# Half products for every second pair of slabs in the FFN up projection, with weight sums made by adding DMAs

## The reference

```python
def conv_ffn(x, w_up, conv_w, conv_b, w_down):
    h = x @ w_up                     # 512 x 1024 @ 1024 x 5632
    h = conv over 3 tokens, per channel, causal, + conv_b
    gate, val = jnp.split(h, 2, axis=-1)
    return (jax.nn.silu(gate) * val) @ w_down
...
x = x + rms_norm(conv_ffn(rms_norm(x, pre_ffn), *ffns[i]), post_ffn)
```

## Time and profile before

| what | value |
|---|---|
| runs | median 2073.37 us of 3 (2070.84 to 2076.74) |
| the profiled execution | 2073.53 us, its span 2071.8 us |
| granted TensorE clock | 0.998 of full speed |
| PE | 2053.4 us busy, 99% of the span |
| DVE | 1413.2 us, 68% |
| ACT | 1023.9 us, 49% |
| POOL | 398.3 us, 19% |
| chain that ended last | PE 85%, DVE 9%, ACT 2%, DMA 2%, issue 1% |
| four stretches of up projection | 165 to 405, 655 to 870, 1220 to 1440 and 1716 to 1935 us, DMA 28% to 32% busy |
| start of the down projection | 405 to 480 us: DVE 69.58 of 75 us busy, DMA 77% |

### The profile page before, as it was taken

How to read it: one execution, slowest core, us unless ns; L and a number is a source line. 1 busy time by engine, 2 the same in 40 slices (tenths; PEclk the granted TensorE clock), 3 DMA queues, 4 the chain that set the end, 5 groups by cost and what they waited for, 6 DMA issues and landing times.

```text
span 2071.8 us, 32448 instructions
## 1 busy us (share of the span) xinstructions
PE 2053.4 (99%) x11724; PEld 1728.4 (83%) x11724; DVE 1413.2 (68%) x2250; ACT 1023.9 (49%) x1671; POOL 398.3 (19%) x454
## 2 busy tenths in 40 slices
PE   9999999999999999999999999999999999999998
PEld 8889888888988888888877898888878889888886
DVE  5665555999366555699788655456987666554897
ACT  4754333557334433456556644334565764333555
POOL 0520211310000121120045401212200520121220
PEclk9999999999999999999999999999999999999999
DMA  8123322384430332267421113233674131233383
GB/s 287 63 102 102 100 88 95 120 262 157 143 132 31 102 101 92 90 189 244 156 72 42 62 41 104 99 101 96 193 229 163 63 103 60 87 98 101 105 265 117
DMA packets 73881, 251.62 MB, mean 121 GB/s; under 512 B 8448, under 2 KB 12672, under 8 KB 73392
## 3 DMA queue, kind: packets, MB, share of 16 engines
q1 hardware_dynamic: 58752, 213.10, 31.2%
q0 software_dynamic: 7168, 16.78, 3.7%
q10 hardware_dynamic: 7856, 20.34, 2.8%
HBM read 248.04 MB, written 6.34 MB: 123 GB/s over the span
## 4 chain that ended last, share of the span: by engine, by line
PE 85%; DVE 9%; ACT 2%; DMA 2%; issue 1%; POOL 0%; DVEq 0%; ACTq 0%; SPq 0%; POOLq 0%
PE ps L2011 16%; PE ps L2013 16%; PE ps L2012 16%; PE ps L2196 6%; PE ps L2530 4%; PE ps L2532 4%; PE ps L2531 4%; PE ps L2083 2%; DMA raw<-slabs 2%; DVE w_lo L1352 2%; PE ps L2039 2%; PE ps L2041 2%; PE ps L2040 2%; PE ps L2071 1%; PE ps L2055 1%; PE ps L2056 1%
## 5 line engine op out<-in xcount | busy, mean ns | idle before, releaser
L2011 PE MATMUL ps<-h_hi,w_hi 128*128 128x512 f32 (+1 forms) x1552 | 606.6, 391 | 0.0
L2012 PE MATMUL ps<-h_lo,w_hi 128*128 128x512 f32 (+1 forms) x1552 | 603.2, 389 | 0.0
L2013 PE MATMUL ps<-h_hi,w_lo 128*128 128x512 f32 (+1 forms) x1552 | 603.2, 389 | 0.0
L1747 DVE SCALAR_TENSOR_TENSOR work<-ps,conv_sb,work 128x511 f32<-128x511 f32 (+1 forms) x352 | 246.2, 744 | 379.4 <-ACT work L1138 379.2
L1352 DVE TENSOR_TENSOR w_lo<-raw,w_hi 128x1024 fp32r<-128x1024 f32 x356 | 439.1, 1240 | 43.6 <-ACT w_hi L777 39.9
L777 ACT ACTIVATE w_hi<-raw 128x1024 fp32r<-128x1024 f32 x368 | 384.5, 1051 | 129.9 <-DVE raw L1836 71.8
L1138 ACT ACTIVATE work<-ps,conv_sb 128x512 f32<-128x512 f32 x176 | 137.0, 778 | 474.7 <-PE ps L2013 445.5
L2011 PEld LDWEIGHTS ps<-h_hi,w_hi 128*128 128x128 f32 x1552 | 291.4, 188 | 62.6 <-issue 4.0
L2013 PEld LDWEIGHTS ps<-h_hi,w_lo 128*128 128x128 f32 x1552 | 291.3, 188 | 60.5
L2012 PEld LDWEIGHTS ps<-h_lo,w_hi 128*128 128x128 f32 x1552 | 291.5, 188 | 58.6
L718 POOL TENSOR_TENSOR bias<-act 128x256 f32<-128x256 f32 x40 | 78.7, 1967 | 996.4 <-DVE act L1753 996.4
(11 more groups left out here) (289 smaller groups left out, 3367.5 us busy)
## 6 DMA issues: line engine op xcount, KB each, us to landing
raw<-slabs SPq DMA_DIRECT2D x368, 512.0 KB, 3.8
act<-slabs POOLq DMA_DIRECT2D x64, 256.0 KB, 5.5
bias<-slabs SPq DMA_DIRECT2D x16, 512.0 KB, 6.1
act<-slabs SPq DMA_DIRECT2D x12, 512.0 KB, 5.7
bias_dram<-bias_rows ACTq DMA_DIRECT2D x2, 2048.0 KB, 13.3
g_post<-gains ACTq DMA_DIRECT2D x8, 512.0 KB, 4.9
bias<-bias_dram ACTq DMA_DIRECT2D x2, 2048.0 KB, 9.6
g_pre<-gains ACTq DMA_DIRECT2D x7, 512.0 KB, 6.9
```

The source lines that it names most:

```text
L1747: ve.scalar_tensor_tensor(y, ps[:, 2 * par + e, 0:SEQ - sh], conv_sb[:, L, t, tap:tap + 1], y, ALU.mult, ALU.add).then_inc(done, 1)
L2011: pe.matmul(ps[:, bank, cols], hi, h_hi[:, k, cols], start=k == 0, stop=False)
L2012: pe.matmul(ps[:, bank, cols], hi, h_lo[:, k, cols], start=False, stop=False)
L2013: last = pe.matmul(ps[:, bank, cols], lo, h_hi[:, k, cols], start=False, stop=k == KT - 1)
```

## The change

In each layer the pairs q = 4, 6, ..., 16 (seven of 22) are made by seven half products. A pair's weights are seen as a 2 x 2 block matrix (output row: gate or value slab; column: first or second half of the 1024 features), the input as 2 x 2 blocks (half of the features; half of the tokens). A half product is 4 k-tiles x 3 matmuls with 256 columns. PE makes them in the order a11, a12, x2, x1, x3, then the whole ordinary slab (q+1, 0), then a22, x4, then the ordinary slab (q+1, 1). This group of two pairs is a `period`. Some products are added onto others in PSUM, so earlier states are copied out by ACT (`copy` 0, 1, 2, 128x256 each) and added back by DVE (`c11`, `c22`, `c12`).

Four sums of weights are needed. DVE makes x2 in SBUF; x1, x3 and x4 are made by DMAs issued by POOL that add onto `raw`: x1 and x3 read the slab from DRAM again, x4 reads x2's place in SBUF. Four differences of the input (`join`, `differ`) are made by DVE at the start of each layer's up projection, split by ACT and DVE (`in_high`, `in_low`) and kept, two of them in the place of x. So x is written to DRAM before (four DMAs of 512 KB on ACT's queue) and read back after pair 18's silu (four more). `down_sums` is called once in each period and not as soon as its pairs are gated. The loops of the stage are written out.

```diff
+FAST, FAST_END = 4, 18
+FASTS = (FAST_END - FAST) // 2
+PARTS = "a11", "x1", "x2", "x3", "x4"
...
-                ring_slabs(n1 + EARLY, DOWN[L] + FFT)
+                ring_slabs(n1 + EARLY, up_slab(L, FAST))
+                for q in range(FAST, FAST_END + 2, 2):
+                    for e in range(2):
+                        c = up_slab(L, q, e)
+                        if q == FAST:
+                            sp.wait_ge(lo_made, made(c - RAW))
+                        elif e:
+                            sp.wait_ge(part_lo_made["x3"], fast(L, q - 2) + 1)
+                            sp.wait_ge(part_lo_made["x4"], fast(L, q - 2) + 1)
+                        else:
+                            sp.wait_ge(part_lo_made["x1"], fast(L, q - 2) + 1)
+                            sp.wait_ge(up_x2, fast(L, q - 2) + 1)
+                        sp.dma_start(raw[:, raw_slot(c), :], slabs[dram(c)]).then_inc(raw_in[raw_slot(c)], 16)
+                    if q < FAST_END:
+                        for e in range(2):
+                            c = up_slab(L, q + 1, e)
+                            sp.wait_ge(lo_made, made(c - RAW))
+                            sp.dma_start(raw[:, raw_slot(c), :], slabs[dram(c)]).then_inc(raw_in[raw_slot(c)], 16)
+                ring_slabs(up_slab(L, FAST_END + 1), DOWN[L] + FFT)
...
+            def up_sums(L):
+
+                def x1(q):
+                    even = up_slab(L, q)
+                    slot = raw_slot(even)
+                    pool.wait_ge(raw_in[slot], raw_count(even))
+                    pool.dma_start(raw[:, slot, 0:SEQ], slabs[dram(even)][:, SEQ:D], accum_op=ALU.add).then_inc(x1_in, 16)
+
+                def x3_x4(q):
+                    row1 = raw_slot(up_slab(L, q, 1))
+                    pool.wait_ge(part_lo_made["a11"], fast(L, q) + 1)
+                    pool.wait_ge(up_x2, fast(L, q) + 1)
+                    pool.dma_start(raw[:, row1, 0:SEQ], slabs[dram(up_slab(L, q))][:, 0:SEQ], accum_op=ALU.add).then_inc(x3_in, 16)
+                    pool.dma_start(raw[:, row1, SEQ:D], sum_place(), accum_op=ALU.add).then_inc(x4_in, 16)
+
+                x1(FAST)
+                for q in range(FAST, FAST_END, 2):
+                    x3_x4(q)
+                    if q + 2 < FAST_END:
+                        x1(q + 2)
+                    down_sums(L, (q - FAST) // 2)
+                for j in range(FASTS, STEPS - 1):
+                    down_sums(L, j)
...
+                def copy(q, n):
+
+                    if n == 2:
+                        sc.wait_ge(w_used, up_slab(L, q) + 2)
+                    else:
+                        sc.wait_ge(up_mm, 5 * fast(L, q) + (1, 3)[n])
+                    if q > FAST:
+                        sc.wait_ge(up_c, 3 * fast(L, q - 2) + (1, 3, 2)[n])
+                    sc.activation(kept_sum(n), ps[:, up_bank(q, 0), 0:HALF], ACT.Copy).then_inc(up_copy, 1)
...
+                def in_high(n):
+
+                    sc.wait_ge(in_sum, 8 * L + 5 + n)
+                    sc.wait_ge(x_out, 16 * TT * (L + 1))
+                    hi, _ = in_parts(n)
+                    sc.activation(hi, whole(*IN_PLACES[n]), ACT.Copy).then_inc(in_hi, 1)
...
+                def period(q):
+
+                    i = q // 2
+                    tap(1, i - 1, 1)
+                    split_hi(up_slab(L, q + 1))
+                    silu(1, i - 1)
+                    copy(q, 0)
+                    part_hi(q, "x3")
+                    split_hi(up_slab(L, q + 1, 1))
+                    copy(q, 1)
+                    part_hi(q, "x4")
+                    copy(q, 2)
+                    if q + 2 < FAST_END:
+                        part_hi(q + 2, "a11")
+                        part_hi(q + 2, "x2")
+                        fast_tap(q, 0)
+                        part_hi(q + 2, "x1")
+                        fast_tap(q, 1)
+                    else:
+                        fast_tap(q, 0)
+                        sc.wait_ge(up_mm, 5 * fast(L, q) + 5)
+                        split_hi(up_slab(L, q + 2))
+                        fast_tap(q, 1)
+                        split_hi(up_slab(L, q + 2, 1))
+                    silu(0, i)
+                    tap(1, i, 0)
...
+                for t in range(TT):
+                    sc.wait_ge(xn_made, TT * (2 * L + 1) + t + 1)
+                    sc.dma_start(x_dram[t], x[:, t, :]).then_inc(x_out, 16)
                 end = FFT // 2 - 1
-                for c in range(2):
-                    pair(c)
-                with sc.Fori(1, end - 1) as i:
-                    for c in range(2):
-                        pair(c, i)
+                pair(0)
+                pair(1)
+                for n in range(4):
+                    in_high(n)
+                tap(0, 1, 0)
+                part_hi(FAST, "x1")
+                tap(0, 1, 1)
+                part_hi(FAST, "a11")
+                silu(0, 1)
+                part_hi(FAST, "x2")
+                tap(1, 1, 0)
+                for q in range(FAST, FAST_END, 2):
+                    period(q)
+                tap(1, end - 2, 1)
+                split_hi(up_slab(L, FAST_END + 1))
+                silu(1, end - 2)
+                split_hi(up_slab(L, FAST_END + 1, 1))
                 pair(0, end - 1)
+                sc.wait_ge(w_used, up_slab(L, FAST_END))
+                for t in range(TT):
+                    sc.dma_start(x[:, t, :], x_dram[t]).then_inc(x_back, 16)
...
+                def period(q):
+
+                    i = q // 2
+                    slab_taps(q - 1, 1)
+                    split_lo(up_slab(L, q + 1))
+                    gate(1, i - 1)
+                    part_lo(q, "x3")
+                    split_lo(up_slab(L, q + 1, 1))
+                    c11(q)
+                    part_lo(q, "x4")
+                    c22(q)
+                    if q + 2 < FAST_END:
+                        x2(q + 2)
+                        part_lo(q + 2, "a11")
+                        part_lo(q + 2, "x2")
+                        slab_taps(q, 0)
+                        c12(q)
+                        part_lo(q + 2, "x1")
+                        slab_taps(q, 1)
+                    else:
+                        slab_taps(q, 0)
+                        c12(q)
+                        split_lo(up_slab(L, q + 2))
+                        slab_taps(q, 1)
+                        split_lo(up_slab(L, q + 2, 1))
+                    gate(0, i)
+                    slab_taps(q + 1, 0)
...
                 end = FFT // 2 - 1
-                for c in range(2):
-                    pair(c)
-                with ve.Fori(1, end - 1) as i:
-                    for c in range(2):
-                        pair(c, i)
+                for n in range(4):
+                    join(n)
+                pair(0)
+                differ(0)
+                differ(1)
+                pair(1)
+                differ(2)
+                differ(3)
+                in_low(0)
+                in_low(1)
+                in_low(2)
+                x2(FAST)
+                taps(0, 1)
+                part_lo(FAST, "x1")
+                gate(0, 1)
+                part_lo(FAST, "a11")
+                in_low(3)
+                part_lo(FAST, "x2")
+                slab_taps(FAST - 1, 0)
+                for q in range(FAST, FAST_END, 2):
+                    period(q)
+                slab_taps(FAST_END - 1, 1)
+                split_lo(up_slab(L, FAST_END + 1))
+                gate(1, end - 2)
+                split_lo(up_slab(L, FAST_END + 1, 1))
...
-                with pe.Fori(1, FFT // 2) as i:
-                    for c in range(2):
-                        pair(c, i)
-
+                def product(q, e, half, name, operand, begin, onto=False):
+                    o = ps[:, up_bank(q, e), HALF * half:HALF * (half + 1)]
+                    (hi, lo), (b_hi, b_lo) = up_parts(L, q, name), operand
+                    for k in range(KT // 2):
+                        w = slice(k * P, (k + 1) * P)
+                        pe.matmul(o, hi[:, w], b_hi[:, k, :], start=begin and k == 0, stop=False, skip_group_check=onto)
+                        pe.matmul(o, hi[:, w], b_lo[:, k, :], start=False, stop=False, skip_group_check=onto)
+                        last = pe.matmul(o, lo[:, w], b_hi[:, k, :], start=False, stop=k == KT // 2 - 1, skip_group_check=onto)
+                    return last
+
+                for c in range(2):
+                    pair(c, 1)
+                for q in range(FAST, FAST_END, 2):
+                    even, f = up_slab(L, q), fast(L, q)
+                    if q >= FAST + 4:
+                        pe.wait_ge(tap0, UP_SLABS * L + 2 * (q - 4) + 2)
+                    pe.wait_ge(part_lo_made["a11"], f + 1)
+                    product(q, 0, 0, "a11", h_quarter(0, 0), True).then_inc(up_mm, 1)
+                    product(q, 1, 0, "a12", h_quarter(1, 0), True).then_inc(up_mm, 1)
+                    pe.wait_ge(up_copy, 3 * f + 1)
```

(65 more changed lines are left out.)

143 lines of the change are left out of this document (129 added, 14 removed).

## The result

The changed kernel takes 2107.1 us (median of 4 runs, 2104.9 to 2110.5), beside 2072.1 us for the kernel before (4 runs, 2070.7 to 2076.7). The ratio is 1.0166, with a 95% interval of 1.0144 to 1.0188: 1.7% slower, where 2065.1 us and a gain of 0.4% were forecast, and outside the forecast range of 2054 to 2084 us. The profiled execution has a span of 2104.8 us; before it was 2071.8 us, so 33.0 us are to be explained.

A forecast was written before the change was run, and what follows sets the result against it. PE was taken to bound the up projection, DVE and the loads behind it its last pairs and the down projection's start. 2073.5 - 22.4 + 7.6 + 6.4 = 2065.1 us, range 2054 to 2084 us for eight in ten.

The forecast's parts named there:

- PE's work: Up projection: seven half products replace an ordinary pair's matmuls, 0.80 us less for each of 28 pairs, 22.4 us less.
- P3 starts at 3.15 instead of 2.88: In each period x2's matmuls wait for ACT's copy 0: 0.27 us lost, 28 times, 7.6 us.
- DVE's list: DVE's work in a period up to x3's low part: ready at 5.1 us, 0.7 us before its use, no wait.
- P5: Fifth half product of a period, x3's matmuls on PE, wanting its low part at 6.03 us.
- rival 2: In each period POOL's sums hold DVE and x3's matmuls wait, up to 1.4 us; 2104 us with all five; 20%.
- The adding DMAs: POOL's DMAs making x1, x3, x4 in the periods: landing after 5.4 to 8.0 us, wanted 10 us later, cost nothing.
- The start of the stage: DVE's input differences at each up projection's start: hidden before PE needs them, cost nothing, 2 us a layer at worst.
- The end of the stage: Behind pair 18, reload of x delays DVE and first down slabs: 1.6 us a layer, 6.4 us in all.
- the bound from the earlier trace with four loads at once: End of the stage: a slab load lands after 6.1 us among four, 3.8 alone, up to 2.3 us later.
- rival 1: End of the stage: reload of x delays first down slabs 2.9 to 5.6 us a layer; 2070 to 2081 us; 20%.
- the three terms: Losses at x3 (forecast nothing), at x2 for ACT's copy (7.6 us) and at the end of the stage (6.4 us).

The follow-up runs named there:

- run 4: Changed kernel with POOL's five sums delayed until c22 and the reload of x moved into the down projection: 2056.7 us, ratio 0.9925.
- run 8: Changed kernel with POOL's five sums delayed until DVE's first split of the period is done, reload untouched: 2075.1 us, ratio 1.0006.
- Runs 2 to 4: Changed kernel with POOL's sums delayed until c22 (2072.2 us), with the reload of x moved into the down projection (2090.2 us), with both (2056.7 us).

## Why the prediction was wrong, step by step

- **PE's work**: right. 128x256 matmuls are 0.120 us apart, and a period without waits is 20.99 us (run 4), where 20.96 was worked out. The 22.4 us are there.
- **"P3 starts at 3.15 instead of 2.88: 0.27 us lost, 28 times, 7.6 us"**: wrong, it is nothing in 26 periods and 0.3 and 0.6 us in two. The tap starts 0.20 us behind the first matmul of the period and not 0.42 as in the earlier trace rows, and the copy takes 0.37 us; it ends at 229.72 + 0.37 = 230.09, 2.71 us into the period, ahead of the 2.88.
- **"DVE's list ... has x3 ready at 5.1, 0.7 us before P5"**: this is the step that failed: the sum put the wait at x3 at nothing, and it is 30.9 us. Undisturbed the step is true (4.88 us in run 4, 0.9 us ahead; by the prediction's own 6.03 for P5 it is 0.9 too, and not 0.7). But it was summed with durations of DVE alone, and the conflict was left to rival 2 with 20%. Rival 2 named place, engine and price: 5 x 0.42 - 0.7 = 1.4 us a period and 2104 us; measured 1.38 us in the second period, 1.29 on average over 24. The price is partly luck: it let each sum in singly for 0.42 us, while the trace shows one hold of 1.55 us by four sums and one of 0.54 us by the fifth. So is the total: 2104 has 39 us for x3, 7.6 for the copy and 6.4 for the end, where 30.9, 0.5 and 22.7 were measured. What was misread is the evidence against it. The 6.47 us of L718 in the earlier trace rows come from a stretch where DVE ran two-input SBUF instructions without a gap and POOL came second. In the period POOL is released during taps, whose input in PSUM doesn't keep it out, so it is POOL that comes first. By the rule of the Trainium skill, "SBUF — State Buffer", section "SBUF: two separate sides", whichever of the two starts first holds the port pair for its whole instruction. It was cited, these rows agree with it in who wins, and so do the turns of run 8, one instruction each. What was not asked is which of the two starts first here. The holds of 6.47 and 1.55 us last over several instructions of the other engine; when a whole train goes through and when the engines alternate, the runs don't tell.
- **The adding DMAs**: hidden, as said. x3's and x4's landed after 4.3 and 5.0 us and PE waits for none. **The start of the stage**: nothing lost, as said.
- **The end of the stage**, "I take 1 us for this and 0.55 for the issues": right in mechanism and place (landing, `first_sum`, passed on to PE), mis-sized. The 0.55 us are nothing: from the three taps ahead of it to the low part of `operand` DVE takes 376.86 - 372.01 = 4.85 us, as before (375.15 - 370.30), since ACT's issues run beside its other work. The landing grew by 3.8 us (7.3 beside 3.5) and not by 1, since the load goes out while most of the 2 MB are still under way, and the DMA engines are 98% busy until it has landed; the bound from the earlier trace rows with four loads at once, 6.1 us, had too few. The fall of the clock behind the wait, 7.8 us, was not in the sum at all. Measured 22.7 us instead of 6.4; by its size this is rival 1 at the top of its span, 5.7 us a layer, but 2 us of them are the clock, which rival 1 did not have.
- **How the cases were combined**: rivals 1 and 2 stood as alternatives, each with everything else at its forecast. They are independent and both came true. Runs 2 to 4 show that they add. With the three terms as measured the prediction's own sum gives 2065.1 + 30.9 - 7.1 + 16.3 = 2105.2 us, beside 2106.5 us of the profiled execution.

## What to carry to other kernels

When work of a second engine is moved in a program, lay its instructions beside the first engine's at the very moment at which they are released, and ask who is under way; a duration taken beside other neighbours says little. Shift the intruder into the other engine's idle time (35 us here) before you reorder its victim (12 us), and keep bulk transfers that nobody is waiting for away from the first load that somebody is. Count independent losses as a sum and not as a choice, and put the lower clock behind a wait of some microseconds into its price.
